# A hybrid recurrent/attention layer with 32 experts: 16 KB weight runs, a reordered opening, gate ratios moved in the head loop

## What is computed

```python
mx = split((silu(c) @ w_mod + b_mod), 6);  mc = split(silu(c_ctx) @ w_mod + b_mod, 6)
hx, hc = modulate(rmsnorm(x, norm1_g), mx[0], mx[1]), modulate(rmsnorm(ctx, norm1_g), mc[0], mc[1])
# one input projection: 9 blocks of 1024 columns; per head of 128 channels:
#   A: centred conv of 4, RG-LRU gates (sigmoid, exp, sqrt), linear scan both ways
#   B: HGRN2 in chunks of 32, both ways, then rmsnorm per head
ox = (sigmoid(ga) * ((ya * gelu(ay)) @ w_proj_a) + sigmoid(gb) * ((yb * silu(og)) @ w_proj_b)) @ w_out
x = x + mx[2] * ox
hx2 = modulate(rmsnorm(x, norm2_g), mx[3], mx[4])
# hier_moe: best of 4 groups, best 2 of its 8 experts, softmax weights
for e in range(32): y += cw[:, e] * ((silu(hx2 @ w1[e]) * (hx2 @ w3[e])) @ w2[e])
return rmsnorm(x + mx[5] * y, final_g)
```

## Time and profile before

| | us |
|---|---|
| median of three runs | 1124.39 (1121.32 to 1124.71) |
| the profiled execution | 1126.62, of which the span is 1124.5 |
| PE busy | 1042.8 (93%) |
| DVE, ACT, POOL busy | 330.7, 374.0, 62.7 |
| DMA moved | 284.13 MB, mean 253 GB/s |
| first head starts on PE | 45.58 |
| first `up` of the experts | 611.04 |
| last expert product ends | about 1108.5 |

### The profile page before, as it was taken

The page is one execution under the profiler, slowest core; times in us unless marked ns, Lnnn a source line. Parts: engine busy times, 40 slices in busy tenths (PEclk is TensorE's granted clock), DMA queues, the critical chain, the costliest instruction groups (busy, mean ns, idle before and its releaser), DMA issues.

```text
span 1124.5 us, 14079 instructions
## 1 busy us (share of the span) xinstructions
PE 1042.8 (93%) x5167; PEld 627.6 (56%) x5168; DVE 330.7 (29%) x793; ACT 374.0 (33%) x668; POOL 62.7 (6%) x107
## 2 busy tenths in 40 slices
PE   2899999999999999999997999999999999999994
PEld 1568686868686868688855444444443334334432
DVE  2245454554554545452214111001101011110013
ACT  5263637373737373730013222222221122122212
POOL 1011111010101010100000000000000000000000
PEclk9899999999989999989997999999999999999997
DMA  9945252525352525208892999999999999999980
GB/s 343 284 112 169 84 168 84 168 84 168 84 168 84 168 84 149 75 8 265 266 396 93 334 380 392 392 394 395 395 395 395 394 392 392 393 395 395 395 337 37
DMA packets 197136, 284.13 MB, mean 253 GB/s; under 512 B 6336, under 2 KB 100736, under 8 KB 197120
## 3 DMA queue, kind: packets, MB, share of 16 engines
q1 hardware_dynamic: 197120, 283.92, 72.4%
HBM read 282.86 MB, written 1.05 MB: 252 GB/s over the span
## 4 chain that ended last, share of the span: by engine, by line
SPq 28%; PE 23%; DMA 2%; DVE 2%; issue 1%; ACT 1%; DVEq 0%; ACTq 0%
SPq L380 28%; PE bank L744 6%; PE bank L474 5%; PE bank L752 3%; PE bank L686 2%; DMA arena<-in_w 2%; PE bank L736 2%; PE bank L762 2%; DVE arena L1411 0%; PE bank L668 0%; PE bank L783 0%; ACT arena L1009 0%; PE bank L696 0%; DVE arena L1241 0%; DVE arena L1422 0%
## 5 line engine op out<-in xcount | busy, mean ns | idle before, releaser
L474 PE MATMUL bank<-arena 128*128 128x256 f32 (+3 forms) x1792 | 405.8, 383 | 5.6 <-DVE arena L1088 5.2
L474 PEld LDWEIGHTS bank<-arena 128*128 128x128 f32 x1792 | 301.2, 192 | 97.6 <-issue 66.9
L744 PE MATMUL bank<-arena 128*64 128x512 f32 x1024 | 231.6, 606 | 14.9 <-DMA arena<-in_w 13.6
L744 PEld LDWEIGHTS bank<-arena 128*64 128x64 f32 x1024 | 74.9, 139 | 168.7 <-issue 153.5
L752 PE MATMUL bank<-arena 128*64 128x512 f32 x512 | 113.4, 595 | 0.0
L995 ACT ACT_TABLE_LOAD x16 | 20.5, 1283 | 214.7 <-PE bank L744 214.7
L1411 DVE TENSOR_TENSOR arena<-arena,bank 128x512 f32<-128x512 f32 x16 | 11.0, 687 | 274.8 <-PE bank L744 274.8
L1415 DVE COPY arena<-bank 128x512 f32<-128x512 f32 x32 | 22.1, 692 | 170.5 <-PE bank L752 170.5
L752 PEld LDWEIGHTS bank<-arena 128*64 128x64 f32 x512 | 35.3, 137 | 65.9 <-issue 64.0
L736 PE MATMUL bank<-arena 128*128 128x128 f32 x544 | 65.8, 281 | 0.6 <-DVE arena L1377 0.6
L736 PEld LDWEIGHTS bank<-arena 128*128 128x128 f32 x544 | 64.2, 197 | 0.7 <-DVE arena L1377 0.7
(11 more groups left out here) (268 smaller groups left out, 909.0 us busy)
## 6 DMA issues: line engine op xcount, KB each, us to landing
arena<-in_w SPq DMA_DIRECT2D x96, 2048.0 KB, 19.7
arena<-in_w_in SPq DMA_DIRECT2D x72, 512.0 KB, 5.1
arena<-in_w_mod SPq DMA_DIRECT2D x12, 2048.0 KB, 8.1
arena<-in_w_proj_a SPq DMA_DIRECT2D x8, 512.0 KB, 4.4
arena<-in_w_proj_b SPq DMA_DIRECT2D x8, 512.0 KB, 5.5
arena<-in_w_out SPq DMA_DIRECT2D x2, 2048.0 KB, 9.7
arena<-in_x SPq DMA_DIRECT2D x4, 512.0 KB, 5.1
arena<-in_ctx SPq DMA_DIRECT2D x2, 512.0 KB, 6.5
```

The costliest lines, as they stand in the source:

```text
L474: i = mm(dst, w(k), rhs(k), start=k == 0, stop=k == KT - 1)
L744: i = mm(acc[SLOTS * b:SLOTS * b + SLOTS, :], xg[:, k, SLOTS * b:SLOTS * b + SLOTS], wslot(kind, b, j)[:, k, :], start=k == 0, stop=k == K ...
```

## The change

Four edits:

- Expert weights: row p*8+k of w1 and w3 (p*4+k of w2) now goes to partition p, so that each partition's 16 KB are one contiguous run in DRAM. The tokens have to follow: `gather` takes every eighth channel (`xn[:, t, kt:D:KT]`, a step of 32 bytes) and the transposes of `gm` every fourth (a step of 16 bytes), both as stationary operands. The second modulation is needed in the same order: at the end of the head loop POOL builds a pattern `spread` and DVE `turned`, PE multiplies them after the router's logits (8 products of 16 columns), and ACT copies the result to `mod_pk`.
- Opening: the twelve parameter loads are issued by ACT. The `w_mod` blocks come in the order 0, 2, 1, 3. PE starts with block 0's rows, and the token transposes stand between the blocks. The modulation is made and applied in two steps, channels of k = 0 to 3 once blocks 0 and 2 are there, the rest at the end.
- Head loop, DVE: ratios(0) goes behind levels(1), then evacuate(0), the modulation add, evacuate(1), and ratios(1) comes after those, just ahead of the scans.
- Head loop, ACT: the two square roots go behind the two activations of `og` and `ga`.

```diff
-        w1_v, w3_v, w2_v = (w[0].rearrange("e (k p) n -> e p k n", p=P) for w in (w1, w3, w2))
+        w1_v, w3_v, w2_v = (w[0].rearrange("e (p k) n -> e p (k n)", p=P) for w in (w1, w3, w2))
...
-            sp.dma_start(wpro[0], wm_v[:, :, 0:512]).then_inc(S("pro_in0"), 16)
-            for i in range(1, 4):
+            for i in PRO_ORDER:
                 sp.dma_start(wpro[i], wm_v[:, :, 512 * i:512 * i + 512]).then_inc(S(f"pro_in{i}"), 16)
...
+            pool.wait_ge(S("inter_mm"), this(HEADS - 1, 1))
+            pool.memset(spread, 1.0).then_inc(S("consts"), 1)
+            keep(spread, 8 * 112, [[-8, 240]], 1).then_inc(S("consts"), 1)
+            keep(spread, 7 - 8 * 112, [[8, 240]], -1).then_inc(S("consts"), 1)
...
             pe.wait_ge(S("csil_out"), 1)
-            for i in range(5):
-                if i < 4:
-                    pe.wait_ge(S(f"pro_in{i}"), 16)
-                    mod_rows(bank[2 + i], wpro[i]).then_inc(S("pro_rows"), 1)
-                if i > 0:
-                    pe.wait_ge(S("pro_part"), i)
-                    ins = mod_sums(bank[6][:, 8 * i - 8:8 * i], 2, wpro[i - 1][:, 0, :])
-            ins.then_inc(S("pro_mm"), 1)
+            pro_rows(0)
+            turn_tokens(0, 4)
+            pro_sums(0)
+            pro_rows(1)
+            turn_tokens(4, KT)
+            pro_sums(1).then_inc(S("pro_rows"), 1)
+            pro_rows(2)
+            pro_rows(3)
+            pe.wait_ge(S("par_copy"), 1)
+            pro_sums(2)
+            pro_sums(3).then_inc(S("pro_mm"), 1)
...
+            pe.wait_ge(S("consts"), 6)
+            pe.wait_ge(S("rt_prep"), 3)
+            for k in range(KT):
+                i = mm(bank[6][:, 0:2 * 8], spread[:, 112 - 16 * k:240 - 16 * k], turned[:, k, :],
+                       start=k == 0, stop=k == KT - 1)
+            i.then_inc(S("rt_mm"), 1)
...
-                        i = mm((GX if half else UX)[:, P * k:P * k + P], xn[:, t, P * kt:P * kt + P],
+                        i = mm((GX if half else UX)[:, P * k:P * k + P], xn[:, t, kt:D:KT],
...
-                    i = pe.transpose(GX[:, P * f:P * f + P], gm[:, P * f:P * f + P], ident[:])
+                    i = pe.transpose(GX[:, P * f:P * f + P], gm[:, f:F:F // P], ident[:])
...
+            i = modulate(2, 4, 6)
...
-                for d in range(2):
-                    act.wait_ge(S("w_out"), this(h, d))
-                    A(tz[d], tz[d], ACT.Sqrt, scale=2.0).then_inc(S("sqrt_out"), 1)
                 act.wait_ge(S("og_mm"), this(h))
                 act.wait_ge(S("yb_out"), last(h))
                 A(sog, PJ[1][:, 0:T], ACT.Silu).then_inc(S("og_out"), 1)
                 A(s_ga[:, h, :], PJ[1][:, T:], ACT.Sigmoid).then_inc(S("ga_out"), 1)
+                for d in range(2):
+                    act.wait_ge(S("w_out"), this(h, d))
+                    A(tz[d], tz[d], ACT.Sqrt, scale=2.0).then_inc(S("sqrt_out"), 1)
...
+            act.wait_ge(S("rt_mm"), 2)
+            A(mod_pk.rearrange("p a b -> p (a b)"), bank[6][:, 0:2 * 8], ACT.Copy).then_inc(S("x1T_out"), 1)
...
                 forget(0)
                 logs(0)
-                ratios(0)
                 prods(0)
                 forget(1)
                 logs(1)
                 levels(0)
-                ratios(1)
                 prods(1)
                 levels(1)
+                ratios(0)
+                evacuate(0)
+                dve.wait_ge(S("mod_mm"), this(h))
+                tt(modB[:, bass.ds(h * 4, 4)], OB[:, 0:4], par2[:, bass.ds(h * 4 + 16, 4)], ALU.add).then_inc(S("mod_out"), 1)
+                evacuate(1)
+                ratios(1)
                 scans(0)
                 scans(1)
...
+            link(dve.tensor_reduce(octet[:], ident[:].rearrange("p (a b) -> p b a", b=8), AX.X, ALU.add))
+            dve.wait_ge(S("inter_mm"), this(HEADS - 1, 1))
+            for n, v in enumerate((modB[:, 8:16], aff2[:])):
+                i = tt(turned[:, :, 8 * n:8 * n + 8], octet[:].unsqueeze(1).to_broadcast([P, KT, 8]),
+                       v.unsqueeze(2).to_broadcast([P, KT, 8]), ALU.mult)
+            i.then_inc(S("rt_prep"), 1)
```

More of the change, by code:

```diff
@@ L57 @@
 UNROLL = 4
+PRO_ORDER = (0, 2, 1, 3)
 A_WBLK = 0
@@ L196, in build @@
         gate1, gate2, fin_g = (at(A_T + 8192 + 1024 * j, D) for j in range(3))
+        spread = at(A_T + 11264, 240)
+        turned = at(A_T + 11504, KT, 2 * 8)
+        mod_pk = at(A_T + 11632, 2, KT)
         diag = at(A_HT + 3072, KT, P)
@@ L236, in wslot, with wtile @@
         def wslot(kind, b, j):
-            s = ring[(6 * j + KINDS.index((kind, b))) % len(RING)]
-            return s.rearrange("p (k n) -> p k n", n=D if kind == "w2" else F)
+            return ring[(6 * j + KINDS.index((kind, b))) % len(RING)]
+        def wtile(kind, b, j):
+            return wslot(kind, b, j).rearrange("p (k n) -> p k n", n=D if kind == "w2" else F)
         ACC = [[bank[0], bank[1]], [bank[2], bank[3]]]
@@ L481, in _, with turn_tokens @@
             pe.transpose(bank[7][:, P:P + 64], prows[0:64, 1, :], ident[0:64, 0:64]).then_inc(S("par_T"), 1)
[L483 to L490, removed]
+            def turn_tokens(first, end):
+                for k in range(first, end):
+                    if k == 0:
+                        pe.wait_ge(S("xs_out"), 4)
+                    if k >= 2:
+                        pe.wait_ge(S("tok_copy"), k - 1)
+                    for t in range(4):
+                        i = pe.transpose(PJ[k % 2][:, P * t:P * t + P], tok[:, t, P * k:P * k + P], ident[:])
+                    i.then_inc(S("tok_T"), 1)
             def mod_rows(dst, w):
@@ L817, in _ @@
             A = act.activation
+            r0 = 0
+            for v, n in rows:
+                act.dma_start(prows[r0:r0 + 8 * n, 0, :], v.rearrange("a (h n) -> (a h) n", n=P)).then_inc(S("par_in"), 16)
+                r0 += 8 * n
+            act.dma_start(prows[0:48, 1, :], b_mod[0].rearrange("(h n) -> h n", n=P)).then_inc(S("par_in"), 16)
+            act.dma_start(prows[48:56, 1, :], c[0].rearrange("(h n) -> h n", n=P)).then_inc(S("par_in"), 16)
+            act.dma_start(prows[56:64, 1, :], c_ctx.rearrange("(h n) -> h n", n=P)).then_inc(S("par_in"), 16)
             for t in range(4):
@@ L832, in _, with rows_part, tokens_out, modulate @@
             A(par[:, V_LBV, :], spt[:, 3, 0:8], ACT.Sigmoid).then_inc(S("sp1"), 1)
[L834 to L847, removed]
+            def rows_part(n):
+                act.wait_ge(S("pro_rows"), n + 1 + n // 2)
+                A(wpro[PRO_ORDER[n]][:, 0, :], bank[2 + n][:], ACT.Copy).then_inc(S("pro_part"), 1)
+            def tokens_out(first, end):
+                for k in range(first, end):
+                    act.wait_ge(S("tok_T"), k + 1)
+                    A(h_ct[:, k, EDGE:], PJ[k % 2][:], ACT.Copy).then_inc(S("tok_copy"), 1)
+            def modulate(step, first, end):
+                act.wait_ge(S("aff1_out"), step)
+                act.wait_ge(S("tok_copy"), KT)
+                for k in range(first, end):
+                    for s in range(2):
+                        i = A(h_ct[:, k, EDGE + T * s:EDGE + T * s + T], h_ct[:, k, EDGE + T * s:EDGE + T * s + T],
+                              ACT.Identity, scale=aff1[:, s, k:k + 1], bias=modA[:, k, s:s + 1])
+                return i
+            rows_part(0)
+            tokens_out(0, 4)
+            rows_part(1)
+            tokens_out(4, KT)
+            rows_part(2)
+            rows_part(3)
+            i = modulate(2, 4, 6)
             i.then_inc(S("h_ct_out"), 1)
```

66 lines of the change are left out of this document (39 added, 27 removed).

## The result

| | us |
|---|---|
| before | 1123.82 (median of 4, 1121.32 to 1124.71) |
| changed | 1143.30 (median of 4, 1140.96 to 1144.01) |
| ratio | 1.0173, 95% interval 1.0151 to 1.0196 |
| profiled execution | 1144.01, span 1142.5 |
| forecast | 1074, range 1063 to 1104 |

The changed kernel's page, 40 slices of 28.6 us. Clock and DMA can be held against the earlier trace rows, where the rate is 392 to 395 GB/s from the 25th slice to the 38th (334 and 380 in the 23rd and 24th). PEclk is the granted clock of TensorE, in tenths of full speed; in windows 1.00 is full speed. The DMA row falls from 9 to 8 in the experts, so DMA waits now; PE's row stays at 9.

What follows compares the result with a forecast made beforehand. It took PE to bound the heads, with a wait and half clock, and weight DMA to bound the later experts. Profiled 1126.6 less 23.6, 5.7 and 21.8 (51.1) gave 1075.5, forecast as 1074 against the median; range 1063 to 1104.

Steps and rivals of the forecast that it cites:

- the price of a strided weight load: Experts' gather loads and transposes, 608 in all: extra cost taken as nothing, with 51 us as the upper end.
- The row that was set aside: DVE's L1233, said to read both inputs in 256-byte steps: 593 ns where L1232 takes 425, 0.66 ns an element.
- The bound itself: Upper end for one strided load in the experts: 128 elements at DVE's 0.66 ns, 84 ns, x 608 = 51 us.
- The working around it: Experts: gather loads have no slack beside a 128-column product, so any growth shows, over 608 loads including 64 transposes.
- Rival (b): Gather and transposes: strided loads at half pace grow by 107 ns, x 608 = 65 us; about 1139 us, chance 0.15.
- The sum of the rest: Whole kernel with strided loads free: 23.6, 5.7 and 21.8 us saved, forecast 1074 us.
- Head loop, 23.6 forecast: Head loop: 11.1 us of PE waits and 12.5 of half clock both go; bounds -11 and -25.
- 11.1 forecast: Head loop: PE's wait of 1.39 us ahead of attention(1) goes in each of 8 heads.
- 12.5: Head loop: us of half clock behind the waits, all taken as gained; 0 if the waits are not its cause.
- Opening, 5.7 forecast: Opening: first head starts at 39.9 us instead of 45.58; -3.5 if PE's chain is late, -7 if nothing is.
- Experts, 21.8 forecast: Experts: 16 KB weight runs at an estimated 425 GB/s make PE the bound, ending at 1086.7 for 1108.5 us.
- the first named sign: Experts: the forecast is wrong if gather takes 7 us; it claimed 3.57 us for 32 records.

Runs made afterwards that it cites:

- e1: The changed kernel with channels reordered once by ACT when it writes xn, so the gather's stationary operand is contiguous, 16 KB runs kept; 1076.22 us, ratio to before 0.9582.
- e4: e1 with the head loop's order of before on DVE and ACT; 1092.76 us.
- e5: e1 with ratios(0) and ratios(1) back at their old places on DVE, the evacuation still ahead of the scans; 1076.01 us.
- e9: e1 with the opening of before on all engines; 1081.26 us.
- e11: The kernel of e1 run again, unchanged, on one chip beside a repeat of e10's kernel; 1076.97 us.
- e10: e1 plus 29 products of bf16 zeros that nobody reads, in two idle stretches of PE in the opening; 1073.29 us, ratio to before 0.9564.
- e3: The changed kernel with the weight layout (2 and 4 KB runs), gather, transposes and modulation of before; 1094.54 us.

## Why the prediction was wrong

**The step that failed** is the one on the price of a strided weight load: "I take nothing, since that row is another engine with far larger steps in pieces of four elements". The measured price is 126 ns for each of 512 gather loads (64.5 us), 1.9 us for the 32 of the first gather, and 0.09 us a pair for the transposes (1.4): 68 us in all. e1, which keeps the strided transposes, got 67 of them back. The row that was set aside, was the right one to follow: DVE's 168 ns over 256 elements are 0.66 ns an element, ACT's read in e1 costs 1046 ns over 1024, 1.02 ns, and PE's 0.95 ns a column (121 over 128). Three engines pay, each at a price of its own. On PE the size of the step had next to no part in it from 16 to 32 bytes: 233, 233 and 237 ns. The bound itself, 84 ns, was too low as well, for it took DVE's price of an element as PE's. (The row was misread in one point: by the program only `hsum`, one input of L1233, is read in steps of 256 bytes, not both.)

The working around it was right for the gather: the load has no slack beside a product of 128 columns. Its record grew by 143 ns, and 126 of them show. It was wrong for the 64 transposes, which it counted at the same price: 22 ns of the 70 show. The point from which the change loses, 84 ns a load, is near: by e1 the rest of the change is worth 48 us, which is 88 ns for each of the 544 gather loads. Rival (b), the load at half pace, gave about 1139 for 1143; its picture is nearly what came, 237 ns a record for 112. No run shows the 107 ns that it adds to a load. At the 112 ns of the records, which it names as the pace, 608 loads would make 68 us and about 1142; measured are 126 ns for a load of the gather and 22 for a transpose. It had 0.15 of the chance, with DVE's row and no slack on PE for it, and against it that this row gives 84 at most. That an unknown has no row is a reason for a wide range, not for the lower end.

**The sum of the rest** was 1074 and is measured in e1, which has no strided load in the gather: 1076.2, 47.6 below the kernel before. Its terms:

- Head loop, 23.6 forecast. The wait goes, and the timeline is as worked out (evacuate(0) ends 0.13 us after `mod_sums` began, 0.7 before PE needs it). e4 gives 16.5. Heads without a drop of the clock are 54.85 apart in e4 and 53.32 in the changed kernel, so the wait is worth 1.5 us a head, 12 in all (11.1 forecast), and some 4 are left for the clock, not 12.5. In the kernel before the clock fell behind the wait in six of eight heads: the granted clock is 0.55 to 0.85 over the 3 or 4 us around these waits and 1.00 around those at 151.64 and 206.47, and the drop shows in the earlier trace rows as 1.19 us for L560, at 0.50 or 0.51, where it is 0.68 at 1.00. It fell in e4's profiled execution in two (1.5 and 1.7 us). The term was sized from one execution, and the clock's part varies: the kernel before, on one chip, took from 1111.86 us at a mean granted clock of 0.981 to 1127.19 at 0.968, and e4's slowest execution, 1103.11, has 0.970 where its fastest has 0.982. For the kernel before, 12.5 may still be right: measured singly, this term (16.5), the opening (4.3 to 5.0) and the experts (18.3) sum to 39 or 40, and e1 lies 47.6 below it. The 8 us between fit the clock that the kernel before lost and e4 didn't, 9.4 against 3.1 us over seven distances between heads, and a drop in the last head that e4 lacks; no run shows this directly.
- The prediction took the moved ratios and the moved evacuation as one edit and didn't ask which of them removes the wait. e5 shows that the ratios' place has no effect. The trace of before had it: levels(1) ended at 428.65, before attention(0) at 429.0.
- Opening, 5.7 forecast, 3.5 in the profiled execution, 5.0 by e9 against e1 and 4.3 on one chip. The fourth block landed when forecast, 32.1. What was left out is the clock behind the 2.4 us in which PE waited for it: 0.8 us in the rows and 1.6 in the sums. The clock falls there in some executions and not in others. In e11's, of e1's kernel, rows and sums took 3.07 and 3.58 us behind 3.04 us of waiting (0.74 over 32 to 34, 0.50 over 34 to 36). No run shows the 1.2 GHz of e10's expectation, only such shares of full speed. In e1's own profiled execution, which has the same opening, rows and sums took 1.92 and 1.95 behind 2.70 us of waiting, at 1.00, and the first head started at 39.82, as forecast:

```profile
32.24 1.92 PE L505 MATMUL bank<-arena 128*32 128x512 f32 x16 [2.70 <-DMA arena<-in_w_mod]
34.09 1.95 PE L512 MATMUL bank<-quad,arena 128*128 128x2 f32 x16
```

- Experts, 21.8 forecast, 18.3 by e3. PE is the bound, as said, with 29.66 us a pair for the 29.54. The rate was sized a little low: 425 GB/s as the estimate, up to 437 measured. With PE as the bound it made no difference.

**What it told right in advance**: gather at 7 us was the first named sign that it was wrong, and is what came (7.60).

**Left open.** The numbers don't say why the clock falls behind one wait of 1.4 us and not behind another of the same length, nor why a strided transpose costs 22 ns where a gather load with the same step costs 121.

## What to carry to other kernels

Before a layout is turned to suit DMA, count who reads it how often: a permutation is to be paid where the data passes once (here two ACT instructions, 2 us beside the router's steps), not in an operand that PE reads in every loop (67 us). In a row of fp32 products of 128 columns, a strided operand was nearly free at a step of 8 bytes (119 ns a record for 112) and took twice the time at 16, 28 and 32 (233 to 237); as moving operand it was tried at 32 bytes only (232), and longer products were not tried. When an edit moves several things, ask of each whether the wait was on it.

## What the hardware showed that was not expected

- fp32 records of PE, a load and a product of 128 columns each, take 112 ns at a step of 4 bytes, 119 at 8, 174 at 12, 233 at 16 and 28, 237 at 32; 232 with the moving operand at 32. In the first gather, at a granted clock of 0.50 for about 4.5 us of it, the step of 32 bytes added 1.9 us and not 4.0. ACT's read of 1024 elements takes 2186 ns at a step of 32 bytes for 1140.
- Expert weights, loads of 2 MB: in runs of 16 KB they reach 431 to 437 GB/s over 10 us, in runs of 4 KB 408, in runs of 2 KB 387. A block of `w_mod` in 2 KB runs reached 412 for 1 us.
- The kernel before, with nothing changed, ran from 1111.86 to 1127.19 us on one chip in ten of eleven executions, and the time followed the mean granted clock, 0.981 to 0.968.
- With products of bf16 zeros in two waits of the opening (2.55 and 4.04 us of them) the granted clock stayed at 1.00 there, and the time was 3.7 us lower (1073.30 for 1076.97).
